# The local attention's probabilities are turned on VectorE and through DRAM instead of on TensorE

## The reference, cut to what matters

```python
def hybrid_layer(x, g, w_in, rpb, ..., w_out, pos):
    h = rms_norm(x, g)
    z = h @ w_in                                   # 29 tiles of 128 output channels
    aq, ak, av, ag, bq, bk, bv, bg, ca, cb, cg = jnp.split(z, splits, axis=-1)
    ya = neighbourhood_attention(heads(aq, 4), heads(ak, 4), heads(av, 4), rpb) * silu(ag)
    yb = dilated_attention(rotary(bq), rotary(bk), bv) * silu(bg)         # 6 heads
    yc = conformer_conv(ca, cb, ...) * silu(cg)
    return x + concat([ya, yb, yc]) @ w_out
```

## Time and profile before

| | |
|---|---|
| median of 3 runs | 536.96 us (536.53 to 539.67) |
| the profiled execution | 538.72 us, of which the span from first to last instruction is 536.7 us |
| granted TensorE clock | 0.995 of full speed |
| busy in the span | PE 521.1 us, PEld 407.0, DVE 369.2, ACT 278.7, POOL 135.7 |
| DMA | 94.41 MB; POOL's queue holds the 16 DMA engines for 50.6% of the span, SP's for 19.4% |

### The profile page before, as it was taken

One profiled execution on the slowest core, in us unless ns is written; L12 is line 12 of the kernel. 1 busy time (PEld: TensorE's weight loads), 2 busy tenths in 40 slices (PEclk: granted clock), 3 DMA queues, 4 the chain that ended last, 5 costly groups with the idle time before them and its releaser, 6 DMA issues.

```text
span 536.7 us, 7774 instructions
## 1 busy us (share of the span) xinstructions
PE 521.1 (97%) x2846; PEld 407.0 (76%) x2846; DVE 369.2 (69%) x721; ACT 278.7 (52%) x535; POOL 135.7 (25%) x168
## 2 busy tenths in 40 slices
PE   8999989999999999999999999999999999799995
PEld 6888767577786878888888877767768688577884
DVE  6889698989974545612639969988998554544034
ACT  6713466566665557634422326764766555554223
POOL 0113332122143312335211323132213331123201
PEclk9999999999999999999999999999999999899999
DMA  8626687767785875899303569967667899769943
GB/s 297 251 79 154 155 202 176 162 165 166 149 202 126 218 169 117 211 280 258 120 0 118 124 144 232 217 145 178 149 166 176 230 220 222 212 152 233 233 70 156
DMA packets 38917, 94.41 MB, mean 176 GB/s; under 512 B 5088, under 2 KB 16608, under 8 KB 38624
## 3 DMA queue, kind: packets, MB, share of 16 engines
q0 software_dynamic: 17856, 61.09, 50.6%
q1 hardware_dynamic: 20736, 32.64, 19.4%
q10 hardware_dynamic: 288, 0.19, 0.2%
HBM read 83.94 MB, written 6.82 MB: 169 GB/s over the span
## 4 chain that ended last, share of the span: by engine, by line
PE 75%; DMA 9%; DVE 9%; issue 2%; SPq 2%; POOL 1%; ACT 1%; POOLq 0%; DVEq 0%; ACTq 0%
PE acc L560 16%; PE acc L562 15%; PE acc L561 15%; PE tp L684 5%; DMA bias<-nabias 4%; PE misc L703 4%; PE sc L670 4%; DMA sq<-sq 3%; DMA v_way<-vB 2%; DVE y L1206 1%; PE sc L622 1%; PE sc L624 1%; PE sc L623 1%; PE sc L560 1%; PE sc L562 1%
## 5 line engine op out<-in xcount | busy, mean ns | idle before, releaser
L560 PE MATMUL acc<-act_hi,w_hi 128*128 128x512 f32 x480 | 195.8, 408 | 0.0
L562 PE MATMUL acc<-act_lo,w_hi 128*128 128x512 f32 x480 | 188.3, 392 | 0.0
L561 PE MATMUL acc<-act_hi,w_lo 128*128 128x512 f32 x480 | 188.0, 392 | 0.0
L562 PEld LDWEIGHTS acc<-act_lo,w_hi 128*128 128x128 f32 x480 | 90.5, 189 | 20.1
L560 PEld LDWEIGHTS acc<-act_hi,w_hi 128*128 128x128 f32 x480 | 90.7, 189 | 17.9 <-issue 1.4
L561 PEld LDWEIGHTS acc<-act_hi,w_lo 128*128 128x128 f32 x480 | 90.8, 189 | 17.2 <-issue 0.5
L783 ACT ACTIVATE w_lo<-w_hi 128x1024 fp32r<-128x1024 f32 (+1 forms) x62 | 61.9, 999 | 43.3 <-DMA w_hi<-w_out 38.3
L846 ACT ACTIVATE prob<-prob,nmx 128x512 f32<-128x512 f32 (+1 forms) x80 | 50.5, 631 | 42.3 <-DVE nmx L1226 42.3
L1206 DVE SCALAR_TENSOR_TENSOR y<-ub,par,y 128x512 f32<-128x512 f32 x90 | 69.7, 774 | 0.0
L853 ACT ACTIVATE prob<-prob,rden 128x512 f32<-128x512 f32 (+1 forms) x80 | 50.4, 630 | 33.3 <-DVE rden L1232 33.0
L1002 POOL DMA_DIRECT2D w_lo<-w_in x40 | 35.7, 893 | 115.6 <-ACT w_lo L783 115.6
(11 more groups left out here) (143 smaller groups left out, 725.6 us busy)
## 6 DMA issues: line engine op xcount, KB each, us to landing
w_hi<-w_in POOLq DMA_DIRECT2D x40, 512.0 KB, 5.7
w_lo<-w_in POOLq DMA_DIRECT2D x40, 512.0 KB, 6.3
w_hi<-w_out POOLq DMA_DIRECT2D x16, 512.0 KB, 6.9
w_lo<-w_out POOLq DMA_DIRECT2D x16, 512.0 KB, 6.5
pT<-w_in SPq DMA_DIRECT2D x15, 512.0 KB, 5.1
bias<-nabias SPq DMA_DIRECT2D x32, 128.0 KB, 5.2
sq<-sq SPq DMA_DIRECT2D x48, 64.0 KB, 2.7
v_way<-vB SPq DMA_DIRECT2D x8, 256.0 KB, 2.8
```

Source lines behind the costliest of these rows:

```text
L560: nc.tensor.matmul(to[:, :], w_hi[:, slot, k, :], a_hi[:, k, :], start=i == 0, stop=False)
L561: nc.tensor.matmul(to[:, :], w_lo[:, slot, k, :], a_hi[:, k, :], start=False, stop=False)
L562: last = nc.tensor.matmul(to[:, :], w_hi[:, slot, k, :], a_lo[:, k, :], start=False, stop=i == K - 1)
```

## The change

For the 16 local units of a layer, TensorE no longer transposes and ScalarE no longer empties. VectorE's `turn_p` transposes the 32 by 32 blocks of `prob` in place of both, into the second half of the unit's row; SP stores two units at a time to DRAM (`store_p`, 8 of 256 KB per layer) and loads four at a time, each of the four partition quadrants from its own columns (`load_p`, 4 times 4 DMAs of 128 KB per layer, in runs of 64 floats). `values` of the local pairs wait for these loads (`p_moved`). Pair 3 moves from slot 34 to slot 38. Pair 4 moves from the end of the slots into the output projection: in layer 0 behind seven eighths of its first tile, in the last layer ahead of the part (0, [3]), the last of the first half. `K_ORDER` puts its y tile last. The x tiles' way through DRAM moves from slots 26 to 36 to slot 33 and later for the first half, and behind everything else for the second.

```diff
-K_ORDER = [2, 3, 4, 0, 5, 6, 1, 7]
+K_ORDER = [2, 3, 4, 0, 5, 6, 7, 1]
...
+        LAST_PAIR = ROW_PARTS[3]
...
+        P_STORES = {DUNITS + LAG + 1 + 2 * s: s for s in range((UNITS - DUNITS) // 2 - 1)}
+        P_LOADS = {30: 0, 34: 1, 38: 2}
+        PV_LOCAL = 38
-        X_BLOCKS = {26: 0, 32: 1}
-        X_STORES, X_LOADS = {27: 0, 34: 1}, {29: 0, 36: 1}
+        X_BLOCKS = {33: 0}
+        X_STORES, X_LOADS = {37: 0}, {39: 0}
...
+            def store_p(l, s):
+                sp.wait_ge(p_blocks, (UNITS - DUNITS) * l + 2 * s + 2)
+                at = 2 * s % PROBS
+                sp.dma_start(p_way[l, 2 * s:2 * s + 2].rearrange("u p c -> p u c"),
+                             prob[:, at:at + 2, NKEY:]).then_inc(p_stored, 16)
+
+            def load_p(l, q):
+                sp.wait_ge(p_stored, 16 * ((UNITS - DUNITS) // 2 * l + 2 * q + 2))
+
+                sp.wait_ge(pv_done, PAIRS * l + DPAIRS)
+                flat = pT[:, :, :, :].rearrange("p r a t -> p (r a t)")
+                t = p_way[l, 4 * q:4 * q + 4].rearrange("u (i p) (j c) -> j p (u i) c", p=BLK, j=QUADS)
+                for j in range(QUADS):
+                    to = flat[BLK * j:BLK * (j + 1), 4 * NKEY * q:4 * NKEY * (q + 1)]
+                    sp.dma_start(to.rearrange("p (b c) -> p b c", b=4 * QUADS), t[j]).then_inc(p_moved[q // 2], 16)
...
+                    if n in P_STORES:
+                        store_p(l, P_STORES[n])
+                    if n in P_LOADS:
+                        load_p(l, P_LOADS[n])
...
+                store_p(l, (UNITS - DUNITS) // 2 - 1)
+                load_p(l, (UNITS - DUNITS) // 4 - 1)
+                if l == LAST:
+                    store_x(1)
+                    load_x(1)
...
-                pe.wait_ge(pt_ready, UNITS * l + UPP * (g + 1))
+                if g < DPAIRS:
+                    pe.wait_ge(pt_ready, DUNITS * l + UPP * (g + 1))
+                else:
+                    pe.wait_ge(p_moved[g - DPAIRS], 2 * MOVED * (l + 1))
...
-                    if n >= UPP + LAG and n % UPP == LAG and n < UNITS + LAG:
+                    if n >= UPP + LAG and n % UPP == LAG and n <= DUNITS + LAG:
                         values(l, n // UPP - 1)
-                    if LAG <= n < UNITS + LAG:
+                    if n == PV_LOCAL:
+                        values(l, DPAIRS)
+                    if LAG <= n < DUNITS + LAG:
                         turn(l, n - LAG)
...
-                values(l, PAIRS - 1)
-
                 if l == LAST:
                     for half, kps in ROW_PARTS:
+                        if (half, kps) == LAST_PAIR:
+                            values(l, PAIRS - 1)
                         row_products(half, kps)
                     break
-                c = N_IN + CT
-                open_tile(l, c)
-                products(c, act_hi, act_lo, order=K_ORDER, ready=(ylo_ready, KD * l))
-                for c in range(N_IN + CT + 1, N_CH):
+
+                for c in range(N_IN + CT, N_IN + CT + 2):
                     open_tile(l, c)
-                    products(c, act_hi, act_lo, order=K_ORDER, used=act_used if c == N_CH - 1 else None)
+                    products(c, act_hi, act_lo, 0, KD - 1, order=K_ORDER, ready=(ylo_ready, KD * l))
+                    if c == N_IN + CT:
+                        values(l, PAIRS - 1)
+                for c in range(N_IN + CT, N_IN + CT + 2):
+                    products(c, act_hi, act_lo, KD - 1, KD, order=K_ORDER, ready=(ylo_ready, KD * l))
...
-                    if n > LAG:
+                    if LAG < n <= DUNITS + LAG:
                         empty_turn(l, n - LAG - 1)
...
+            def turn_p(l, n):
+
+                dve.wait_ge(p_ready, UNITS * l + n + 1)
+                u = n - DUNITS
+                if u >= PROBS:
+                    dve.wait_ge(p_stored, 16 * ((UNITS - DUNITS) // 2 * l + (u - PROBS) // 2 + 1))
+                t = prob[:, n % PROBS, :]
+                nc.vector.transpose(t[:, NKEY:].rearrange("p (j h t) -> p h j t", j=QUADS, t=BLK),
+                                    t[:, 0:NKEY].rearrange("p (h j t) -> p h j t", j=QUADS, t=BLK)).then_inc(p_blocks, 1)
...
+                    if DUNITS + LAG <= n < UNITS + LAG:
+                        turn_p(l, n - LAG)
...
                 if l == LAST:
+                    turn_blocks(1)
                     break
```

More of the change, by code:

```diff
@@ L103 @@
 X_GROUPS = [(0, 1), (1, 2), (2, 3), (3, 5), (5, 6), (6, 8)]
-X_ORDER = [list(range(KD))] + [K_ORDER] * (DEPTH - 1)
+X_ORDER = [list(range(KD))] + [[2, 3, 4, 0, 5, 6, 1, 7]] * (DEPTH - 1)
 WARM = 10
@@ L250, in build @@
         p_ready = sem("p_ready")
+        p_blocks = sem("p_blocks")
+        p_stored = sem("p_stored")
+        p_moved = [sem(f"p_moved{i}") for i in range(PAIRS - DPAIRS)]
         t_ready = sem("t_ready")
@@ L420, in quadrant, with local @@
             return t.rearrange("(i p) (j c) -> j p i c", p=BLK, j=QUADS)[j]
+        def local(u):
+            flat = pT[:, :, :, :].rearrange("p r a t -> p (r a t)")
+            return flat[:, NKEY * u:NKEY * (u + 1)].rearrange("p (i h t) -> p i h t", i=QUADS, t=BLK)
         def x_turned(half):
@@ L678, in turn @@
                 pe.wait_ge(p_ready, UNITS * l + n + 1)
-                if UNITS * l + n:
-                    pe.wait_ge(pt_ready, UNITS * l + n)
-                blocks = QT if g < DPAIRS else NKEY // P
-                for k in range(blocks):
+                if DUNITS * l + n:
+                    pe.wait_ge(pt_ready, DUNITS * l + n)
+                for k in range(QT):
                     last = nc.tensor.transpose(tp[:, k * P:(k + 1) * P],
@@ L710, in values @@
                                                         v_of(g, i, na_block(b, half)),
-                                                        pT[:, BLK * i // HD, half, b * P:(b + 1) * P],
+                                                        local(UPP * (g - DPAIRS) + 2 * b + BLK * i // HD)[:, :, half],
                                                         start=half == 0, stop=half == 1)
@@ L762, in _ @@
                         norm_bc(l, MISC_LBC, 2 * l + 2)
-                values(l, PAIRS - 1)
                 if l == LAST:
                     for half, kps in ROW_PARTS:
+                        if (half, kps) == LAST_PAIR:
+                            values(l, PAIRS - 1)
                         row_products(half, kps)
                     break
-                c = N_IN + CT
-                open_tile(l, c)
-                products(c, act_hi, act_lo, order=K_ORDER, ready=(ylo_ready, KD * l))
-                for c in range(N_IN + CT + 1, N_CH):
+                for c in range(N_IN + CT, N_IN + CT + 2):
                     open_tile(l, c)
-                    products(c, act_hi, act_lo, order=K_ORDER, used=act_used if c == N_CH - 1 else None)
+                    products(c, act_hi, act_lo, 0, KD - 1, order=K_ORDER, ready=(ylo_ready, KD * l))
[3 more added lines that the diff above has]
+                    products(c, act_hi, act_lo, KD - 1, KD, order=K_ORDER, ready=(ylo_ready, KD * l))
+                for c in range(N_IN + CT + 2, N_CH):
+                    open_tile(l, c)
+                    products(c, act_hi, act_lo, order=X_ORDER[l + 1], used=act_used if c == N_CH - 1 else None)
         @block.scalar
@@ L1359, in _ @@
                         reciprocal(l, n - 1)
-                    if n > UPP + LAG and n % UPP == LAG + 1 and n < SLOTS - 1:
+                    if DUNITS + LAG <= n < UNITS + LAG:
+                        turn_p(l, n - LAG)
+                    if n > UPP + LAG and n % UPP == LAG + 1 and n <= DUNITS + LAG + 1:
                         gated(l, n // UPP - 1)
+                    if n == PV_LOCAL + 1:
+                        gated(l, DPAIRS)
                     j, phase = divmod(n - LN_SILU, 2)
```

16 lines of the change are left out of this document (9 added, 7 removed).

## The result

The changed kernel took 578.0 us (median of 4 runs, 574.41 to 579.61), the kernel before 536.75 beside it (4 runs): a ratio of 1.0742, 95% interval 1.0712 to 1.0773. The forecast was 543.0 with a range up to 552. The direction was right, the size was not: +39.9 us of span (576.6 for 536.7), where the sum said +6.4.

A forecast was written before the change was run, and what follows sets the result against it. TensorE bounds the local slots while SP's queue is quick. -9.3 (turns) - 6.8 (layer 1's waits) + 12.0 (local slots) + 1.5 (pair 4, layer 0) + 9.0 (last layer) = +6.4 us, from 536.96 to 543.4; range 531.5 to 552.

The forecast's parts named there:

- TensorE bounds the local slots as long as SP's queue is quick: Main reading of the local slots: with about 4 MB more in SP's queue, this ends.
- Part 4's balance of free engine time: Local slots: stores and loads need 13.4 to 20.0 us per layer; 14.5 (layer 0) and 9.1 (layer 1) are free.
- the rival of engines that run out: DMA engines lack time in layer 0's slots and in the last layer: +16, 553 us, chance 0.13.
- Part 1: Local slots: 32 turns leave TensorE at 0.29 us each, saving 9.3 us.
- Part 3: Local slots: VectorE's block transposes take 0.4 us each, 6.4 us per layer, hidden in its idle time.
- Part 4's price: SP's queue: 256-byte packets cost between 13 and 26 ns each, the new loads 6.7 to 13.3 us per layer.
- the rival at 573 us: Probabilities' loads: a small packet costs twice the 26 ns, +36, 573 us, chance 0.02.
- Part 5: Local slots: bias loads wait in SP's queue behind the probabilities' loads, losing 6.0 us per layer (1 to 8).
- Part 6: Layer 0, pair 4's values: TensorE waits 1.5 us (0 to 4) for the probabilities' store and loads.
- Part 7's chain: Last layer, behind pair 4's values: TensorE idle for gated, y_hi, negate and accumulating load, 9.0 us (6 to 12.6).
- Its late weights: Last layer: weights of tiles 6 to 8 start later, 0 to 3 us late, taken as 0.
- x's second half: Last layer: x's second half arrives 20 us after pair 4's values, needed after 28; hidden, with 3 us to spare.

The follow-up runs named there:

- runs 4 and 7: Four bias buffers instead of two, each loaded two units earlier: on the changed kernel (stores' semaphore also split) 561.1 us, on the kernel before 532.5 us.
- run 3: Changed kernel with the probabilities loaded in contiguous runs of 4 KB instead of 256 bytes, same bytes but blocks misplaced: 570.8 us.
- run 1: Changed kernel with ScalarE negating the last layer's last three output weights ahead of pair 4's y_hi: 568.1 us.
- Run 2: Kernel before, turns kept on TensorE, with only pair 4's values moved to their new place: 552.0 us.
- run 5: Changed kernel with ScalarE's negate of the second output tile's weights moved behind y_hi(6) in both layers: 572.7 us.
- run 10: Changed kernel with four bias buffers, early negates in the last layer, OUT0's accumulating load first, and OUT1's negate behind the high halves: 552.2 us.

## Why the prediction was wrong

The places that it named were right, and so was the direction. What failed is the sum: 33.5 us are missing. It has no term for the first output product (9.4 us), whose weights had landed under pair 4's values at their old place and now also landed later; none for the clock behind the new waits (10.5 us net), and 1.5 us for pair 4 in layer 0, where 6.6 were waited. Its own signs of too low a forecast both came: a wait for `p_moved` (6.5 us) and late weights in the second half of the rows (3.4 us).

- **The reading "TensorE bounds the local slots as long as SP's queue is quick"** was right, and runs 4 and 7 show it more sharply: TensorE stood without a wait at 0.94 and 0.96 of the DMA engines' time, so the limit was how early the bias is asked for. Part 4's balance of free engine time, and the rival of engines that run out, argued with the wrong quantity for these slots. In front of the output products the added traffic did cost, as below.
- **Part 1** was mis-sized: 6.6 us, not 9.3. One pair of turns was read, and over a whole stretch a turn is 0.21 us.
- **Part 3** was right: `turn_p` took 0.43 us, and VectorE had room.
- **Part 4's price** held: from 184.5 to 187.5 us, in the row of SP's queue below, 0.363 x 16 x 3.0 us / 842 packets = 21 ns, nearly all of 256 bytes, between the 13 and 26. The Trainium skill (DMA: Bandwidth & Descriptors, section Specifications) has transfers under 512 bytes miss line rate. The trace agrees, for 256 bytes in 21 ns are 12 bytes per ns and 512 in 26 ns are 20; but a packet that took twice the 26 ns, the rival at 573 us, is not what it shows. That the time came out near that rival's is chance.

```profile
q1 hardware_dynamic: 842, 0.21, 36.3%
```

- **Part 5** was right in the waits, 7.1 and 5.3 us for 6.0 in each layer, and failed by the clock behind them, which took another 3.4 us in each. It did not have that issuing four loads itself holds SP, 7.6 us in layer 0; but run 3, where they took 2.2, has the same waits.
- **Part 6** failed by size, 6.6 us for 1.5. It put one store, one load and their landings behind the last `turn_p`, 10 to 12 us. The trace has 20: the store of the last two units landed after 9.2 us and the last load after 8.9. In run 3, with long runs, the same two took 4.3 and 7.1, the chain 13, and TensorE did not wait, though POOL's weight loads held the engines for 77% of the time from 223 to 233 us there and 81% here. So most of what the 10 to 12 us lacked came with the small packets. The chain:

```profile
222.99 9.15 DMA p_way<-prob
...
232.52 0.72 SPq L515
...
233.87 8.93 DMA pT<-p_way
```

- **Part 7's chain** was right in place and size: 8.3 us for 9.0. Its late weights, taken at 0 of 0 to 3, were 3.4 us and hung on the same order (run 1).
- **What no part had** is the first output product, 9.4 us. Moving the values away from the end of the slots took some 2.4 us of TensorE's work from in front of it (2.0 the values, 0.4 the last two turns), under which its weights had landed: before, OUT0's load landed within 0.2 us of that product in layer 1 already. The prediction costed what the values would meet at their new place, and not what they covered at the old one. That is the smaller part. Run 2, with the values moved alone, waits 0.7 and 2.2 us there, the changed kernel 3.1 and 5.9. Most of the rest fits OUT0's accumulating load, which took 8.5 and 10.6 us to land and not 5.4 and 6.8. In the last layer SP's queue moved nothing during that load before (479.6 to 486.4 us), and now took 43.9% of the engines' time (498.2 to 508.9 us), with x and the probabilities:

```profile
q1 hardware_dynamic: 1992, 1.20, 43.9%
```

- **The clock** was in no term of the new waits: it cost 10.5 us more than before, 5.1 of it in the local slots, 3.5 in the output parts and 1.9 under pair 4's values in layer 0.
- **x's second half** was hidden, by less than it seemed: its row sums began at 558.08, after 24 us of waiting for x, and had caught up by the last ones (1.1 us idle before each, for TensorE).

```profile
558.08 2.48 DVE L1484 TENSOR_TENSOR pT<-sc,x 128x512 f32<-128x512 f32 x4 [24.15 <-DMA x<-x_way]
...
570.33 0.69 DVE L1484 TENSOR_TENSOR pT<-misc,x 128x512 f32<-128x512 f32 x1 [1.08 <-PE misc L664]
```

Open: 0.6 us of the span, why OUT0's load landed sooner in run 5, and how much lead the bias needs for no wait in any execution.

## What to carry to other kernels

When an instruction is moved, cost the place that it leaves: what landed under it there is now waited for. A DMA queue that one engine issues in order is judged by the lead of its most urgent small load, and not only by how full the DMA engines are; here 128 KB buffers two units deeper were worth 17 us in one kernel and nearly 6 in the other. And a wait on TensorE can cost more than its length: look in the rows for the clock behind it. Here that was a quarter of the loss.

## What the hardware showed unexpectedly

- A DMA issue on SP's queue took 0.3 to 4.9 us. Four loads of 2048 packets in all (256 bytes each) in a row took 7.6 us to issue, 9.0 in run 10, and with long runs 2.2.
- 256-byte packets cost 21 ns (184.5 to 187.5 us, beside POOL's weight loads), 512-byte ones in the trace before 26 ns (with little beside them): half the bytes saved a fifth of the price.
- The length of a wait did not tell what clock would follow it. Matmuls ran 0.43 us apart, at a granted clock of 0.50, after 3.3 us idle (from 195.69), after 5.9 us (from 509.0), and after only 1.3 us (205.9 to 209.0); after 3.1 us idle at 231.30 they ran 0.23 us apart, at 1.00 from 231.3 to 236.0.
- A 512 KB accumulating load, OUT0's in the last layer, landed in 6.8 us before and in 10.6 after, with 1.2 MB on SP's queue beside it (x and the last probabilities).
